# Turning half of each convolution tile on VectorE, with four smaller moves, in a float32 two-block network on one core

## What is computed

```
def _causal_depthwise_conv(x, w, b):          # x (1, 256, 4096), w (4, 4096), b (4096)
    y = conv(x, w, padding=(3, 0), one filter per feature)
    return y + b
qk = silu(_causal_depthwise_conv(concatenate([q, k]), conv_w, conv_b))
q, k = qk[..., :2048], qk[..., 2048:]         # 8 heads of 256
```

```
lr = (hn @ w_in)[..., -32:]                   # two directions, rank 16
gk = lr @ w_gate_up + b_gate                  # then log_sigmoid, cumulated over chunks
```

## Time and profile before

| what | value |
|---|---|
| median of 3 runs | 2220.8 us (2220.54 to 2221.08) |
| the profiled execution, its own time | 2220.5 us |
| its span, first to last instruction | 2218.4 us |
| TensorE, matmuls | 2204.7 us busy, 99% |
| VectorE | 1530.7 us busy, 69% |
| ScalarE | 1063.2 us busy, 48% |
| GpSimd | 30.7 us busy |
| DMA | 413.96 MB, mean 187 GB/s |

### The profile page before, as it was taken

How to read it: one execution, slowest core, us unless ns; L and a number is a source line. 1 busy time by engine, 2 the same in 40 slices (tenths; PEclk the granted TensorE clock), 3 DMA queues, 4 the chain that set the end, 5 groups by cost and what they waited for, 6 DMA issues and landing times.

```text
span 2218.4 us, 27603 instructions
## 1 busy us (share of the span) xinstructions
PE 2204.7 (99%) x10028; PEld 1828.3 (82%) x10028; DVE 1530.7 (69%) x2213; ACT 1063.2 (48%) x1332; POOL 30.7 (1%) x45
## 2 busy tenths in 40 slices
PE   9999999999999999999999999999999999999998
PEld 7888888888888888888888888888888888888887
DVE  6887797877766447777778746777555559645865
ACT  5564455544444334444445645444445555543443
POOL 0000000000000000000000100000000000000000
PEclk9999999999999999999999999999999999999999
DMA  8654476666666666666666656565755556666653
GB/s 270 181 166 118 134 223 191 197 191 197 190 196 192 192 196 190 196 192 190 187 216 189 202 152 190 173 200 170 208 179 163 171 162 200 199 194 207 195 190 114
DMA packets 283180, 413.96 MB, mean 187 GB/s; under 512 B 21071, under 2 KB 146395, under 8 KB 282555
## 3 DMA queue, kind: packets, MB, share of 16 engines
q1 hardware_dynamic: 282062, 408.55, 60.8%
q10 hardware_dynamic: 1008, 3.94, 0.5%
HBM read 410.33 MB, written 2.10 MB: 186 GB/s over the span
## 4 chain that ended last, share of the span: by engine, by line
PE 91%; issue 0%; DVE 0%; ACT 0%; DVEq 0%; POOLq 0%; POOL 0%; ACTq 0%
PE acc L1211 29%; PE acc L1212 29%; PE acc L1213 29%; PE mx L1360 1%; PE tp L1229 1%; PE mx L1401 1%; PE tp L1373 0%; PE tp L1374 0%; PE tp L1375 0%; PE mx L1189 0%; PE mx L1188 0%; PE mx L1190 0%; PE tp L1417 0%; PE tp L1414 0%; PE tp L1266 0%
## 5 line engine op out<-in xcount | busy, mean ns | idle before, releaser
L1551 DVE TENSOR_TENSOR w_lo<-raw,w_hi 128x1024 fp32r<-128x1024 f32 x768 | 937.4, 1224 | 575.5 <-ACT w_hi L766 571.8
L766 ACT CAST w_hi<-raw 128x1024 fp32r<-128x1024 f32 x768 | 802.5, 1048 | 930.5 <-PE acc L1213 910.9
L1211 PE MATMUL acc<-w_hi,xa_hi 128*128 128x512 f32 x2240 | 880.0, 393 | 0.0
L1213 PE MATMUL acc<-w_hi,xa_lo 128*128 128x512 f32 x2240 | 872.2, 389 | 0.0
L1212 PE MATMUL acc<-w_lo,xa_hi 128*128 128x512 f32 x2240 | 871.8, 389 | 0.0
L1213 PEld LDWEIGHTS acc<-w_hi,xa_lo 128*128 128x128 f32 x2240 | 420.4, 188 | 88.4
L1212 PEld LDWEIGHTS acc<-w_lo,xa_hi 128*128 128x128 f32 x2240 | 420.8, 188 | 85.1
L1211 PEld LDWEIGHTS acc<-w_hi,xa_hi 128*128 128x128 f32 x2240 | 420.7, 188 | 85.0
L1211 PE MATMUL acc<-w_hi,xb_hi 128*128 128x512 f32 x384 | 150.1, 391 | 0.4 <-DVE w_lo L1551 0.2
L1213 PE MATMUL acc<-w_hi,xb_lo 128*128 128x512 f32 x384 | 149.5, 389 | 0.0
L1212 PE MATMUL acc<-w_lo,xb_hi 128*128 128x512 f32 x384 | 149.4, 389 | 0.0
(11 more groups left out here) (289 smaller groups left out, 1191.5 us busy)
## 6 DMA issues: line engine op xcount, KB each, us to landing
raw<-in_w_in SPq DMA_DIRECT2D x192, 512.0 KB, 3.9
...
raw<-in_w_in SPq DMA_DIRECT2D x128, 256.0 KB, 3.0
...
```

Source lines behind the costliest of these rows:

```text
L766: nc.scalar.copy(w_hi[:, hl, 0:kc * job.w], raw[:, slot, 0:kc * job.w]).then_inc(hi_ready, 1)
L1211: nc.tensor.matmul(a[t][:, 0:w], xh, hi, start=first, stop=False)
L1213: ins = nc.tensor.matmul(a[t][:, 0:w], xl, hi, start=False, stop=last)
L1551: nc.vector.tensor_tensor(w_lo[:, hl, 0:kc * job.w], raw[:, slot, 0:kc * job.w], w_hi[:, hl, 0:kc * job.w].bitcast(F32), ALU.subtract) \
```

## The change

1. Convolution tiles 1 to 7 of qk2 (tile 0 stays as it was): TensorE turns only the first two of the four feature pieces, one per bank, 4 matmuls in place of 8. The other two are turned by VectorE within stage (turn_qk2), four instructions of 32x128 at each of granules 4 to 7, which wait for the transposes of the same round. ScalarE evacuates both token halves at j = 3. The first tap with the bias is ScalarE's (first_tap): at j = 6 for the half in PSUM, at j = 0 of the next tile for the half in stage. VectorE's other three taps (taps) stand at j = 6, and at j = 0 and 1 of the next tile. silu follows in halves (half_silu).
2. The first granule is split in two of one row block each; the side work of the first tile moves by one j with it, x is turned one pair per granule, there are 8 dummies instead of 10, and constants_after keeps its own j.
3. The low-rank round (lr_folded, lr_back and what reads them) and gk_piece come one granule later; the evacuation of tile 0 waits for rstd instead of for that round.
4. A_LO and A_ROWS go from 32 and 40 to 64 and 72.
5. The turns of key tile 3 stand in blocks in v0 and v1, instead of one per granule in v1 and v2.

The diff, cut to its core:

```
 LO_ROWS, HI_ROWS = 32, 64
-GK_AT = 11
-X_TURNED_AT = {0: (0, 1), 1: (2,), 2: (3,), 3: (4,), 4: (5,), 5: (6,), 6: (7,)}
+GK_AT = 12
+X_TURNED_AT = {0: (0,), 1: (1,), 2: (2,), 3: (3,), 4: (4,), 5: (5,), 6: (6,), 7: (7,)}
 GATE_ROWS = HI_ROWS + RANK + 1
...
 VW = 258
-A_LO, A_ROWS = 32, 40
+A_LO, A_ROWS = 64, 72
 POOL_WINDOWS = (2, 4, 8, 16)
...
     jobs = [
-        Job("qk", 1, full + granules(16, 16)), Job("qk", 3, full, first=1), Job("v", 4, full), Job("og", 4, full),
+        Job("qk", 1, [(0, 1), (1, 1)] + full[1:] + granules(16, 16)), Job("qk", 3, full, first=1), Job("v", 4, full), Job("og", 4, full),
         Job("wo", 4, full),
...
         KEY_TURNS = {("qk", 3, 5): (2, 0, 4), ("qk", 3, 7): (2, 4, 8), ("v", 0, 0): (2, 8, 12), ("v", 0, 2): (2, 12, 16)}
-        KEY_TURNS.update({("v", 1 + u // 8, u % 8): (3, u, u + 1) for u in range(16)})
+        KEY_TURNS.update({("v", 0, 6): (3, 0, 4), ("v", 0, 7): (3, 4, 6), ("v", 1, 0): (3, 6, 10), ("v", 1, 1): (3, 10, 14),
+                          ("v", 1, 2): (3, 14, 16)})
...
             return stage[:, :, HF:NC].rearrange("p f (t a c) -> p t f a c", t=2, c=32)[:, :, :, a, :]
+        def qk2_blocks(b):
+            return stage[:, :, HF:NC].rearrange("p t (f b c) -> p t f b c", f=2, c=32)[:, :, :, b, :]
+        def qk2_turned_blocks(a):
+            return stage[:, :, 0:HF].rearrange("p f (t a c) -> p t f a c", t=2, c=32)[:, :, :, a, :]
+        def qk2_behind(name, n):
+            return n - 2 if name == "qk2" else 6 + n if name == "v2" and n < 2 else -1
...
-            return 8 * n + j if name == "qk" and j < 8 else -1
+            return 8 * n + j if name == "qk" and n else -1
...
                     sp.dma_start(diag2[:, :], c_diag).then_inc(loads["diag"], 16)
-                if j == 0:
+                if j == 1:
                     load_x_pair(1)
-                if j in (1, 2, 3):
-                    load_x(j)
+                if j in (2, 3, 4):
+                    load_x(j - 1)
...
                     src = a[0][:, 0:w]
-                    if name in ("qk", "qk2"):
+                    if name == "qk2" or name == "qk" and n:
                         act.wait_ge(tp_ready, stage_free(job, n))
+                    if name == "qk2" and n >= 2:
+                        act.wait_ge(taps_done, n - 1)
+                    elif name == "qk":
+                        act.wait_ge(rstd_ready, 1)
                     if name == "qk" and n == 3:
...
                     nc.scalar.activation(dst, src, ACT.Copy, scale=scale).then_inc(evac[0], 1)
+                    if name == "qk2" and n:
+                        nc.scalar.activation(stage[:, 1, :], a[1][:, :], ACT.Copy, scale=rstd[:, S2, 1:2]) \
+                            .then_inc(evac[1], 1)
                 elif name == "zb":
...
+            def first_tap(n, half):
+                act.wait_ge(qk2_ready, 2 * n - 1 + half)
+                if half:
+                    act.wait_ge(qk2_turned, n)
+                else:
+                    act.wait_ge(tp_ready, 2 * (J["qk2"].r0 + n) + 2)
+                for f in range(2):
+                    k = 4 * n + 2 * half + f
+                    src = stage[:, f, 0:HF] if half else tp[f][:, 0:T]
+                    nc.scalar.activation(conv[:, 2 * half + f, :], src, ACT.Identity, scale=cw[:, 96 + k:97 + k],
+                                         bias=cbias[:, k:k + 1]).then_inc(tap_ready, 1)
+            def half_silu(n, half):
+                if half:
+                    act.wait_ge(taps_done, n)
+                else:
+                    for b in range(2):
+                        act.wait_ge(tp_read[b], J["qk2"].r0 + n + 1)
+                nc.scalar.activation(qk2T[:, 4 * n + 2 * half:4 * n + 2 * half + 2, :],
+                                     conv[:, 2 * half:2 * half + 2, :], ACT.Silu).then_inc(qk2_ready, 1)
             def qk2_silu(n):
...
                     gla_squares(after_head(name, n))
-                if name == "qk2" and n >= 2 and j == 0:
-                    qk2_silu(n - 2)
-                if name == "v2" and n < 2 and j == 0:
-                    qk2_silu(6 + n)
+                behind = qk2_behind(name, n)
+                if behind == 0 and j == 0:
+                    qk2_silu(0)
+                if behind > 0 and j == 0:
+                    half_silu(behind, 0)
+                    first_tap(behind, 1)
+                if behind > 0 and j == 4:
+                    half_silu(behind, 1)
                 if name == "oz" and n >= 1 and j == 1:
...
                     evacuate_transposed(pj, pn)
+                if pj is not None and pj.name == "qk2" and pn and j == 6:
+                    first_tap(pn, 0)
                 if (name, n, j) == ("f2o", 0, 7):
...
                 elif name in ("qk", "qk2", "pm"):
-                    transpose_round(r, lambda f, t: stage[:, t, f * P:(f + 1) * P])
+                    transpose_round(r, lambda f, t: stage[:, t, f * P:(f + 1) * P], 1 if name == "qk2" and n else 2)
                 elif name in ("og", "wo", "f2o", "pg"):
...
                     pooled(j + 1)
-                if (name, n, j) == ("qk", 1, 0):
+                if (name, n, j) == ("qk", 1, 1):
                     lr_folded()
-                if (name, n, j) == ("qk", 1, 1):
+                if (name, n, j) == ("qk", 1, 2):
                     lr_back()
...
                             if j == 0:
-                                keep_busy(10)
+                                keep_busy(8)
                         if token_halves_apart(job, n, j):
...
                 a = acc_of(job, ns)
-                if name in ("zb", "gb", "ga", "pool"):
+                if name in ("zb", "gb", "ga", "pool") or name == "qk2" and n:
                     return
...
                     src = a[1][:, 0:w]
-                    if name in ("qk", "qk2"):
+                    if name == "qk2" or name == "qk" and n:
                         dve.wait_ge(tp_ready, stage_free(job, n))
+                    elif name == "qk":
+                        dve.wait_ge(rstd_ready, 1)
                     if name == "qk" and n == 3:
...
+            def turn_qk2(n, a):
+                for t in range(2):
+                    dve.wait_ge(evac[t], E(J["qk2"], n))
+                dve.wait_ge(tp_ready, 2 * (J["qk2"].r0 + n) + 2)
+                if n >= 2:
+                    dve.wait_ge(taps_done, n - 1)
+                own = slice(32 * a, 32 * a + 32)
+                for b in range(4):
+                    ins = nc.vector.transpose(qk2_turned_blocks(a)[32 * b:32 * b + 32], qk2_blocks(b)[own])
+                if a == 3:
+                    ins.then_inc(qk2_turned, 1)
+            def taps(n, half, features):
+                for f in features:
+                    dve.wait_ge(tap_ready, 4 * (n - 1) + 2 * half + f + 1)
+                if half:
+                    dve.wait_ge(qk2_turned, n)
+                else:
+                    dve.wait_ge(tp_ready, 2 * (J["qk2"].r0 + n) + 2)
+                for tap in (2, 1, 0):
+                    s = 3 - tap
+                    for f in features:
+                        k = 4 * n + 2 * half + f
+                        src = stage[:, f, 0:HF - s] if half else tp[f][:, 0:T - s]
+                        own = conv[:, 2 * half + f, s:T]
+                        ins = nc.vector.scalar_tensor_tensor(out=own, in0=src, scalar=cw[:, tap * 32 + k:tap * 32 + k + 1],
+                                                             in1=own, op0=ALU.mult, op1=ALU.add)
+                        if tap == 0 and not half:
+                            ins.then_inc(tp_read[f], 1)
+                    if tap:
+                        settle(ins)
+                if half and 1 in features:
+                    ins.then_inc(taps_done, 1)
             def convolve(n, b):
...
                     mix(j + 1)
-                if pj is not None and pj.name == "qk2" and j in (6, 7):
+                if pj is not None and pj.name == "qk2" and pn == 0 and j in (6, 7):
                     convolve(pn, j - 6)
-                if (name, n, j) == ("qk", 0, 7):
+                if qk2_behind(name, n) > 0 and j < 2:
+                    taps(qk2_behind(name, n), 1, (j,))
+                if pj is not None and pj.name == "qk2" and pn and j >= 4:
+                    turn_qk2(pn, j - 4)
+                if pj is not None and pj.name == "qk2" and pn and j == 6:
+                    taps(pn, 0, (0, 1))
+                if (name, n, j) == ("qk", 0, 9):
                     gate_weights(0)
...
                     gate_weights(1)
-                if (name, n, j) == ("qk", 1, 4):
+                if (name, n, j) == ("qk", 1, 5):
                     lr_transposed()
...
```

37 lines of the change are left out of this document (19 added, 18 removed).

## The result

| what | before | the change |
|---|---|---|
| median of the runs | 2220.67 us (2220.19 to 2221.08) | 2237.44 us (2236.71 to 2241.01) |
| ratio | | 1.0079, 95% interval 1.0066 to 1.0092 |
| span of the profiled execution | 2218.4 us | 2235.9 us |
| mean granted clock | 1.000 | 0.997 |

A forecast was written before the change was run, and what follows sets the result against it. TensorE's products were taken to bound the kernel, at full clock. Against 2220.5 us the terms -3.1 + 16.0 - 2.2 - 1.2 + 0.5 + 0 gave +10.0: 2230.5 us, range 2224.0 to 2236.0.

The forecast's parts named there:

- The chain on VectorE: Convolution tiles: VectorE's turns, w_lo and taps queue behind a first turn waiting for transposes; TensorE waits 2.29 us per tile.
- Product 7 starts at S + 10.89: S is the start of transposes after granule 3; granule 7's product was forecast there instead of at S + 8.60.
- w_lo 5 is ready at S + 3.15 against 3.16 needed, level to 0.15: Granule 5's low weight part, counted in us from the transposes' start S, was forecast to be just in time.
- The clock falls: Rival, 2%: after each of seven waits one granule runs at 1.2 GHz, 2.72 us more each, total 2249.5 us.
- the 0.92 us stand at the folded matmuls: TensorE's wait in the old kernel's low-rank matmuls, with mean clock 1.000; cited against a clock fall.
- The start: First tile: earlier first product from the split granule, lost to the changed SP queue; +0.5 us, bounds -1.0 and +2.0.
- one place further back, the first of them should land near 20.9: First tile: granule of rows 8, 9, behind the constants in the queue, lands near 20.9 us; its product starts at 23.3.
- The pick: The heads' pick matmul with 72 rows instead of 40: 0.28 us less in eight heads, -2.2 us, bounds 0 and -2.8.
- Low-rank round: Four small matmuls one granule later find VectorE's copies ready: -1.2 us, bounds -0.5 and -1.6.
- transposes: Convolution tiles: seven rounds go from eight transposes to four, saving TensorE 0.44 us each, -3.1 us.
- key turns: Sixteen turns regrouped into blocks: 0 us in all, bounds -1.3 and +1.7, with 0.9 lost at the queries' product.
- the waits: TensorE's waits for w_lo ahead of granule 7 in seven convolution tiles, 2.29 us each, +16.0 us.

The follow-up runs named there:

- turns_late: The change with VectorE's four turns at granules 6 and 7 (two each) instead of 4 to 7, PSUM taps behind the last turn; 2215.14 us, ratio 0.9979.
- turns_from5: The change with VectorE's turns at granules 5 (two), 6 and 7 instead of 4 to 7; 2224.06 us, ratio 1.0016.
- turns_at4: The change with all sixteen turns of a tile at granule 4; 2256.87 us, ratio 1.0166.

## Why the prediction was wrong, by its steps

**The chain on VectorE was right to a few hundredths.** "Product 7 starts at S + 10.89": measured 10.90. "w_lo 5 is ready at S + 3.15 against 3.16 needed, level to 0.15" erred by 0.2: VectorE's turn began 0.73 behind S, not 0.63, and product 5 started 0.16 late, with a first matmul 0.11 longer. That shares the loss out between two places, 2.05 and 0.26, and leaves the sum at 2.31 where 2.29 was forecast. The 10.90 owes something to two errors that cancel: w_lo 7 ended at S + 10.84 in place of 10.75, and TensorE started 0.06 behind it in place of 0.14. A tile took 24.7 us without a fall of the clock (24.5 were forecast) and 26.3 with one. turns_late shows the cause for itself: take the w_lo out from behind the blocked turn, and the loss is gone.

**The clock was the step that failed.** The rival "The clock falls" had 2% and a price of 19 us, one granule at half pace after each wait. Its mechanism came true at 3 of the 7 waits and cost 4.8 us, 1.6 each and not 2.72. The mistake was in the evidence against it: the 0.92 us stand at the folded matmuls was taken to speak for a wait of 2.3 us. turns_from5 shows seven waits of about that length (1.09) without a fall, and turns_at4 seven of 3.9 to 4.0 with one each; the forecast's own waits were between them. Three falls of 1.6 in the sum would have given 2235.3, still inside the range, and as a bound they belonged in it; the measured time less these 4.8 is 2232.6.

**The start was mis-sized: +0.5 forecast with +2.0 as the bound, +2.4 measured.** The order of the queue was read rightly, but the step "one place further back, the first of them should land near 20.9" counted bytes at 402 GB/s. The loads that moved ahead run at about 150 GB/s, and they also slowed the granule in front of them in the queue, which the sum left out: rows 6, 7 were split from 17.08 in place of 14.4, rows 8, 9 were split from 22.02 in place of the 20.9 forecast, and the product forecast for 23.3 started at 25.27. The 402 GB/s were read at 8 to 10 us, from another kind of load.

**The pick** was mis-sized the other way, -2.2 against -2.9: the 0.28 of the step was right, the 0.10 that the scores behind it save was not counted. **Low-rank round** (-1.2) and **transposes** (-3.1) came out as worked; **key turns** at -0.1, with the wait at head 0 at 1.0 against 0.9.

The forecast and the measurement are 2237.4 - 2230.5 = 6.9 us apart: +4.8, +0.8 and +0.5 behind the waits, +1.9 at the start, +0.2 for the waits, -0.1 for the keys, -0.7 at the pick. That makes 7.4, against 17.5 - 10.0 = 7.5 in the profiles. The range was too narrow above all for one reason: it summed the bounds of known terms and left the clock, which could only add, out of it. The start also came out 0.4 beyond its own bound.
